# Layer 0's and the third layer's output projections in split operands, weights streamed for every block, and a bias table spread from DRAM to DRAM

## The reference

```python
# layer 0
o_a = rms_norm(diff_attention(..., rel_bias[:, :A_HEADS]), subln_g) * (1.0 - lam_init)
o_b = dsa_attention(..., rel_bias[:, A_HEADS:], top_k)
mix = jnp.concatenate([o_a, o_b], axis=-1)
return x + (mix * jax.nn.silu(gate)) @ w_o          # e_w_o, 1024 x 1024
# third layer (second block)
y_f = fourier_mix(u_f, w_fourier[l], b_fourier[l])
y_a = windowed_gqa(q, k, v, rel_bias, sink[l])
mixed = jnp.einsum('bse,ed->bsd', jnp.concatenate([y_f, y_a], axis=-1), w_out[l])
x = x + g1 * mixed
```

## Time and profile before

| | us |
|---|---|
| runs without a profile, median of 3 | 2521.23 |
| lowest and highest | 2519.8 and 2523.14 |
| the profiled execution, whole | 2521.95 |
| its span | 2520.0 |
| PE busy in it | 2331.1 |

### The profile page before, as it was taken

How to read it: one execution, slowest core, us unless ns; L and a number is a source line. 1 busy time by engine, 2 the same in 40 slices (tenths; PEclk the granted TensorE clock), 3 DMA queues, 4 the chain that set the end, 5 groups by cost and what they waited for, 6 DMA issues and landing times. The chain is left out here.

```text
span 2520.0 us, 35443 instructions
## 1 busy us (share of the span) xinstructions
PE 2331.1 (93%) x13159; PEld 1785.8 (71%) x13159; DVE 1737.0 (69%) x3255; ACT 1341.5 (53%) x2161; POOL 666.3 (26%) x586
## 2 busy tenths in 40 slices
PE   7789999899998999999998989989992999999998
PEld 6476887555655987777777878766661888888886
DVE  4899998768773325666776355336656888888886
ACT  5445312455554375556655242445443877777774
POOL 2345320111110000767678400002315121122210
PEclk9989999799998999999999989989995999999999
DMA  4232221210102332233333331211116999999995
GB/s 151 34 69 59 84 76 56 79 51 30 47 26 84 113 76 62 75 87 84 84 113 95 124 142 38 89 63 35 34 52 256 389 387 392 390 383 384 384 395 182
DMA packets 171320, 362.40 MB, mean 144 GB/s; under 512 B 44056, under 2 KB 91880, under 8 KB 171152
## 3 DMA queue, kind: packets, MB, share of 16 engines
q1 hardware_dynamic: 147344, 308.52, 33.7%
q0 software_dynamic: 23504, 51.48, 8.2%
q10 hardware_dynamic: 304, 0.15, 0.0%
HBM read 321.23 MB, written 38.82 MB: 143 GB/s over the span
## 5 line engine op out<-in xcount | busy, mean ns | idle before, releaser
L994 ACT ACTIVATE a_pT<-ps 128x512 f32<-128x512 f32 (+3 forms) x176 | 79.8, 484 | 181.6 <-PE ps L872 180.3
L1904 DVE MAX8 l_best<-sel 128x8 f32<-128x640 f32 (+5 forms) x176 | 162.8, 925 | 6.1
L1905 DVE MATCH_REPLACE8 sel<-l_best,sel 128x640 f32<-128x640 f32 (+5 forms) x176 | 159.5, 906 | 0.0
L3660 POOL DMA_INDIRECT out_dram<-m_q,e_token x15 | 34.0, 2266 | 447.4 <-DVE m_q L3858 447.4
L1006 ACT ACTIVATE a_p<-ps,a_stat 128x384 f32<-128x384 f32 (+7 forms) x192 | 129.0, 673 | 19.6 <-DVE a_stat L1085 13.7
L2659 ACT ACTIVATE l_lat<-ps,h_stat 128x384 f32<-128x384 f32 (+7 forms) x128 | 94.2, 740 | 76.9 <-DVE h_stat L2849 40.0
L919 PE MATMUL ps<-l_wo,a_mixT 128*128 128x512 f32 x256 | 119.9, 594 | 0.9 <-DVE a_y L2043 0.9
L2239 POOL TENSOR_TENSOR ada_acc<-ada_acc,ada_w 128x384 f32<-128x384 f32 x112 | 116.8, 1042 | 8.8
L2669 ACT ACTIVATE h_pT<-ps 128x512 f32<-128x512 f32 (+2 forms) x192 | 83.5, 490 | 58.9 <-PE ps L2542 58.9
L3489 DVE TENSOR_TENSOR x_w2l<-x_raw,x_w2h 128x4096 fp32r<-128x4096 f32 x23 | 101.8, 4425 | 18.4 <-ACT x_w2h L3481 18.4
L3489 DVE TENSOR_TENSOR x_w1l<-x_raw,x_w1h 128x4096 fp32r<-128x4096 f32 x23 | 101.8, 4425 | 16.1 <-ACT x_w1h L3481 16.1
(11 more groups left out here) (700 smaller groups left out, 7029.6 us busy)
## 6 DMA issues: line engine op xcount, KB each, us to landing
x_raw<-in_w_gate SPq DMA_DIRECT2D x25, 2048.0 KB, 11.5
x_raw<-in_w_down SPq DMA_DIRECT2D x24, 2048.0 KB, 10.9
x_raw<-in_w_up SPq DMA_DIRECT2D x23, 2048.0 KB, 11.9
ada_w<-in_w_ada POOLq DMA_DIRECT2D x64, 384.0 KB, 3.8
m_ufT<-in_w_up SPq DMA_DIRECT2D x9, 2048.0 KB, 12.3
m_ufT<-in_w_down SPq DMA_DIRECT2D x8, 2048.0 KB, 13.0
l_raw<-in_e_w_in SPq DMA_DIRECT2D x28, 512.0 KB, 4.0
m_ufT<-in_w_gate SPq DMA_DIRECT2D x7, 2048.0 KB, 10.4
```

The source lines that it names most:

```text
L1904: link(nc.vector.max(best[:], line))
L1905: link(nc.vector.match_replace(line, best[:], line, TAKEN))
```

## The change

Four things.

1. *The table of biases.* SP writes the 20 rows to a small DRAM tensor `rel_rows_d`, and then five DMAs of four heads each repeat them from DRAM to DRAM (`spread_rows`). Three are issued before the loads of QA1, G0 and G1, two between the stores of the first two strips of w_o and the gate stores. POOL issues none.
2. *Layer 0's w_o is split once and put in DRAM.* Four strips O0 to O3 of 256 columns of `e_w_o` go through the same raw tiles, ACT and POOL as the other strips, have no groups on PE, and are stored as high and low halves (1 MB each) to `wo_d`. The gate strips G2 and G3 come before KA0 now.
3. *Layer 0's pieces in split operands* (`StreamedOut`). For each block SP loads 16 units of 512 KB (high and low part of one piece's weights) into a ring of seven; three fp32r matmuls a piece. The left side is split in two halves a block, each with a copy on ACT and a subtraction on DVE. POOL now loads the x rows and stores the result rows.
4. *Chunks 0 to 3 of the third layer in split operands.* The weights are split in the Fourier stage (four copies on ACT, four subtractions on DVE); the left side with a copy on ACT and a subtraction on DVE for each block.

The core of the diff:

```diff
+    def store_out(e, n):
+        e.wait_ge(pr.lows, 2 * pr.place[OUT[n]] + 2)
+        for part, x in enumerate(out_room):
+            e.dma_start(t.wo_d[n // 2, :, :, part, n % 2 * 256:n % 2 * 256 + 256].rearrange("c p n -> p c n"), x[:].bitcast(F32)).then_inc(wo_out, 16)
+    def rows_to_dram(e):
+        e.wait_ge(tables.ready, 2)
+        e.dma_start(t.rel_rows_d[0:12], t.bias_rows[0:12, :]).then_inc(rows_sent, 16)
+        e.dma_start(t.rel_rows_d[12:20], t.bias_rows[32:40, :]).then_inc(rows_sent, 16)
+    def spread_rows(e, n):
+        table, h = divmod(4 * n, 12)
+        e.wait_ge(rows_sent, 32)
+        e.dma_start((t.rel1_d, t.rel2_d)[table][h:h + 4],
+                    t.rel_rows_d[4 * n:4 * n + 4, :].unsqueeze(1).broadcast_to([4, P, REL_LEN])).then_inc(rel_out[table], 16)
...
-            for i in (VA1, KB, QA0, QA1, G0, G1, KA0):
+            rows_to_dram(e)
+            pr.load(e, VA1)
+            pr.load(e, KB)
+            pr.load(e, QA0)
+            for n, i in enumerate((QA1, G0, G1)):
+                spread_rows(e, n)
                 pr.load(e, i)
-            gate.store(e, 0)
-            pr.load(e, KA1)
-            gate.store(e, 1)
+            for n, (out, later) in enumerate(zip(OUT, (G2, G3, KA0, KA1))):
+                pr.load(e, out)
+                pr.load(e, later)
+                store_out(e, n)
+                if n < 2:
+                    spread_rows(e, 3 + n)
+                gate.store(e, n)
...
-                    if n % 3 == 0 and n // 3 - 3 < len(PIECES):
-                        rel_piece(e, *PIECES[n // 3 - 3])
...
+class StreamedOut:
+    RING, HALF, UNITS = 7, KD // 2, 2 * KD
+    def load(self, e, at, n, h, c):
+        g = self.UNITS * n + KD * h + c
+        if g == 0:
+            e.wait_ge(self.wo_out, 128)
+        if g >= self.RING:
+            half, chunk = divmod(g - self.RING, KD)
+            self.unit_done(e, at, half // 2, half % 2, chunk)
+        i, _ = self.place(n, h, c)
+        e.dma_start(self.ring[i][:].bitcast(F32), self.t.wo_d[h, c]).then_inc(self.unit_in[i], 16)
+    def pe(self, e, n, h, c):
+        if h == 0 and c % self.HALF == 0:
+            e.wait_ge(self.mix_lows, 2 * n + c // self.HALF + 1)
+        i, times = self.place(n, h, c)
+        e.wait_ge(self.unit_in[i], 16 * times)
+        high, low = self.ring[i][:, 0, :], self.ring[i][:, 1, :]
+        for part, (x, w) in enumerate(((self.mix_h, high), (self.mix_h, low), (self.mix_l, high))):
+            last = self.nc.tensor.matmul(self.t.ps[:, 7, :], x[:, c, :], w, start=c == part == 0, stop=c == KD - 1 and part == 2)
...
+            for n in range(NB):
+                for q in range(split.UNITS):
+                    split.load(e, at, n, *divmod(q, KD))
+                    if q in (4, 6) and n + 1 < NB:
+                        at.load_gate(e, n + 1, q // 2 - 2, t.gateT_d)
...
+                    at.store(e, n - 1, t.x1_d)
+                    if n + 1 < NB:
+                        load_rows(e, n + 1)
...
+                for c in {1: (0, 1), 2: (2, 3)}.get(p, ()):
+                    e.wait_ge(wo_in, 32)
+                    nc.scalar.activation(wo_high[:, c, :], wo[:, c, :], ACT.Copy).then_inc(wo_highs, 1)
```

More of the change, by code:

```diff
@@ L915, in pe_pieces @@
                 self.chunk_ready(e, n, c)
-            if self.split and c >= self.split.FIRST:
+            if self.split:
                 last = self.split.pe(e, n, h, c)
@@ L1207, with __init__ @@
     FIRST = KD // 2
-    def __init__(self, k, t, raw):
+    def __init__(self, k, t, first, fixed, still):
         self.nc, self.t = k.nc, t
-        self.raw = [x.rearrange("p (c n) -> p c n", n=D) for x in raw]
-        self.high, self.low = (k.sb(f"w_wo{part}", [P, KD // 2, D], F32R) for part in "hl")
+        self.first_high, self.first_low = first
+        self.fixed, (self.fixed_h, self.fixed_l) = fixed, still
+        scope = k.scope
+        self.high = k.sb("w_woh", [P, KD // 2, D], F32R)
+        with ExitStack() as under:
+            k.scope = under
+            self.raw = k.sb("w_wo_raw", [P, KD // 2, D])
+        k.scope = scope
+        self.low = k.sb("w_wol", [P, KD // 2, D], F32R)
         self.mix_h, self.mix_l = (k.sb(f"w_mix{part}", [P, KD // 2, P], F32R) for part in "hl")
@@ L1243, in act @@
             e.wait_ge(self.raw_in[u // 2], 16)
-            self.nc.scalar.activation(self.high[:, u, :], self.raw[u // 2][:, u % 2, :], ACT.Copy).then_inc(self.highs, 1)
+            self.nc.scalar.activation(self.high[:, u, :], self.raw[:, u, :], ACT.Copy).then_inc(self.highs, 1)
         elif u % at.per == 0:
             self.act_mix(e, at, u // at.per - 1)
+        if u % at.per == at.per - 1:
+            n = u // at.per
+            if n:
+                e.wait_ge(self.fixed_used, n)
+            self.nc.scalar.activation(self.fixed_h[:], self.fixed(at.order[n]), ACT.Copy).then_inc(self.fixed_highs, 1)
     def dve(self, e, at, u):
@@ L1270, in __init__ @@
         self.pick = k.sb("r_pick", [P, EXPERTS])
+        scope = k.scope
+        with ExitStack() as under:
+            k.scope = under
+            self.under_shift = [k.sb(f"w_fixed{part}", [P, KD // 2, P], F32R) for part in "hl"]
+        k.scope = scope
         self.shift = k.sb("r_shift", [P, KD, P])
@@ L1444, in layer0 @@
             early = IndexRoom(k)
+        with ExitStack() as later:
+            k.scope = later
+            k.sb("l0_qi_pad", [P, 4, SEQ])
+            out_room = [k.sb(f"l0_wo_{part}", [P, KD, 256], F32R) for part in "hl"]
         k.scope = persist
@@ L1812, in _ @@
             e.dma_start(bias[:, :, :], offset_bias(t.rel1_d, range(12), P, 2 * P)).then_inc(b_in, 16)
-            pr.load(e, G2)
-            pr.load(e, G3)
-            gate.store(e, 2)
-            gate.store(e, 3)
         @block.gpsimd
```

190 lines of the change are left out of this document (134 added, 56 removed).

## The result

The changed kernel takes 2529.93 us in the median of 15 runs (2523.66 to 2534.64), the kernel before, on the same chips, 2521.31 (15 runs, 2516.31 to 2526.22). The ratio is 1.0033, interval 1.0025 to 1.0041: slower by a third of a per cent, where 2510 was forecast and the range ended at 2526. The profiled execution took 2526.13 us, with a span of 2524.3.

What follows compares the result with a forecast made beforehand. PE was taken as the limit in layer 0's and the third layer's attention, DVE's top-k as the projection's floor. +6 - 8.5 - 9.5 + 0.5 = -11.5 from 2521.95 gave 2510; range 2500 to 2516, with rivals 2493 to 2526.

Steps and rivals of the forecast that it cites:

- Table pieces leave POOL: Layer 0 projection: weights of strip KB land sooner, PE gains 26.5 us, by itself worth only 3.0.
- DVE's 429.3: Layer 0 projection: DVE's last top-k ends at 429.3 us, a floor that no gain of PE goes under.
- Strips of w_o in the projection: Layer 0 projection: late gate stores cost PE 32.5 us; PE ends at 438.3, the projection costs 6 us more.
- Rival B: Projection: gate stores wait longer, from a spread of about 19 us on; at 24.6, +24 and 2528 in all; chance 0.17.
- A: Projection: the spread is quick or its wait covered; -3 instead of +6, 2501 in all; chance 0.20.
- Layer 0's output pieces: Layer 0 attention: shorter split pieces give 12 us, copies take 5, the tail gives 1.6; -8.5 in all.
- two subtractions on DVE (0.68): Layer 0 block changes: part of the copies' cost, 1.3 us each with ACT's copies; 7 blocks at 0.7, minus 5.
- +3 if block changes eat the rest: Layer 0 attention: the slower bound of the step put at -8.5 us.
- Tail: End of layer 0's attention: sixteen shorter pieces give 2.6 us, POOL issuing the last store costs about 1; net 1.6.
- I cost it at nothing; its cover is that lead: Layer 0 attention's weight stream: seven ring places lead by 19 us on the mean, 13 in small blocks; cost nothing.
- Rival D: Layer 0 attention: the ring runs dry in small blocks, 0.5 us in 16 units, +8, 2518; chance 0.05.
- Third layer and Fourier: Third layer attention: 64 shorter pieces less new copies, -9.5 us; Fourier stage: ACT's four copies, +0.5.

Runs made afterwards that it cites:

- e2: Changed kernel, but SP issues each gate store as soon as due and the table spreads last: 2523.32 us, ratio 1.001 to the kernel before.
- e8: Changed kernel with POOL subtracting low halves, gate stores when due, SP issuing the last store, last half product in float32: 2515.15 us.
- e9: Changed kernel with POOL's addition waiting, gate stores when due, SP's last store, last half product in float32 with loads in order of need: 2505.85 us.
- e10: Kernel before plus the third layer's part and the table spread by SP from DRAM; no streamed weights: 2510.12 us, ratio 0.9949.
- e11: Changed kernel, but the left side is split for the first block alone and reused: 2511.62 us in one round, loop 336.9.
- e1: Changed kernel, but POOL's addition of x waits for DVE's first low-half subtraction of the next block: 2518.42 us, ratio 0.9992 to the kernel before.
- e12: Changed kernel, but POOL's addition of x is replaced by a MEMSET of the same shape: loop 343.1 us, whole time 2515.8 in one round.
- e4: Changed kernel, but the last block's pieces 7 to 15 reload no weights: 2522.33 us, ratio 0.9999 to the kernel before.
- e6: Changed kernel, but SP instead of POOL issues the store of the last block's rows: 2527.99 us, ratio 1.0025 to the kernel before.
- e3: Kernel before with the third layer's part of the change alone: 2512.29 us, ratio 0.9962.

## Why the prediction was wrong

**Table pieces leave POOL.** The mechanism held (KB in 2.8 us, no gap at 136). Of the 26.5 us of PE's gain, 22 are there: PE ends at 410 where nothing holds it (e2, e8, e9, e10) and at 432.3 before. Of the 4.5 that are missing about 3 lie in a new short gap: in the kernels with the table spread by SP, PE stands 1.5 us before 174 to 177, and in the changed kernel the granted clock is 0.72 from 174 to 180. The 3.0 us that this was to be worth alone are not: DVE's 429.3 was taken as fixed, and in e10 DVE ended at 433.7, held up by POOL as the loop is.

**Strips of w_o in the projection.** Right in mechanism and place. The loss of PE was put at 32.5, it is 436.9 - 410 = 27; the gain was 4.5 too large as well, so the errors nearly cancel, and 438.3 became 436.9: the sum is closer than its terms by luck. The spread, taken at 13, costs 11. Rival B didn't come: it needed 19. Nor did A: it needed a quick spread, on all 16 engines, and there were four.

**Layer 0's output pieces.** This is the step that failed. Its gain in the units was right (12 said, 11.7 in e11), and the copies' own cost nearly so (5 said, 6.4). What the step left out is in its sentence "two subtractions on DVE (0.68)": the duration was taken from the third layer and carried to a place where POOL adds 128x1024 of x at just that moment. There it is 2.7 us, six times, with PE behind it: 11.6 us (e1, e12). The rows that gave the 0.68 held the warning, and I did not look at their neighbours. POOL's addition stands there too; the instruction of DVE just ahead of the subtraction is held up by it, and the subtraction starts as it ends. In the trace of before, POOL's additions in layer 0, then the third layer: DVE's copies there, and one block change:
```profile
L2001 POOL TENSOR_TENSOR a_y<-a_y,l_xb x7: 2346/2350/2357, 527.5 to 781.2; 128x1024 f32<-128x1024 f32 x7
...
L1108 DVE COPY a_over<-a_stat x29: 226/227/2268, 1693.1 to 1861.6; 128x128 f32<-128x128 f32 x29
...
1749.55 2.35 POOL L3353 TENSOR_TENSOR m_ufT<-m_ufT,w_xb 128x1024 f32<-128x1024 f32 x1
1749.72 2.26 DVE L1108 COPY a_over<-a_stat 128x128 f32<-128x128 f32 x1
1751.91 0.68 DVE L1239 TENSOR_TENSOR w_mixl<-a_mixT,w_mixh 128x512 fp32r<-128x512 f32 x1
```
Median 0.23, longest 2.27, at six block changes: a duration whose longest is ten times its median asks for its neighbours. The copy reads one SBUF tile, so the clash is not one of instructions with two SBUF operands alone. The old layer 0 had no long operation of DVE that started at that moment, so its rows gave only clean ones. The bound of the step was "+3 if block changes eat the rest"; the loop alone reached +6.3.

**Tail.** Also failed: -1.6 was said, +7.6 came. "I cost it at nothing; its cover is that lead" holds in the loop, where PE never waited for the ring, and not in the tail, which the sentence did not look at: sixteen pieces in 11 us ask for 750 GB/s, the queue gave 407. e4 gives its price, 7.0 us, of which the three waits are 1.15 + 1.69 + 1.56 = 4.4 and most of the rest is the low clock behind them; e6 gives 3.1 for the store by POOL, where about 1 was booked. So the step as a whole missed by 22.4 us (-8.5 said, +13.9 measured), and the runs hold nearly all of it: 11.6 for the clash, 7.0 for the dry ring, 2.1 for the store, 1.4 for the copies. Rival D had the mechanism (a dry ring), but in the wrong place.

**Third layer and Fourier.** -9.5 said, -9.4 measured, and again -9.5 in e3; Fourier +0.5 said, -1.4 measured, and no run was made on that.

Profile against profile the change costs 4.2 us, by the medians 8.6. The stages above sum to 4.1. The rest stays open: the profiled execution of the changed kernel lies 3.8 below its median, first scores vary from 435.8 to 440.5 in the seven other kernels whose projection is the same, and the stage of layer 2 takes 767.3 here but 770 to 772 in seven of the ten other kernels with streamed weights (mostly in its attention). No run was made on it.

## What to carry over

A duration may be carried to another place only with its neighbours: look what POOL reads at the moment at which a DVE instruction starts, at the old place and at the new one, and look at the longest, not the median, of its kind. Held up here were DVE instructions with two SBUF operands (0.69 to 2.7 us), but a copy and a TENSOR_SCALAR with one as well. A streamed operand has to be priced where the consumer is fastest, which is the tail, and there the order of loads on one queue must be the order of need. Where PE is given back time ahead of a stage whose end another engine sets, expect none of it, and ask what the earlier PE moves beside that engine.

## What was not expected of the hardware

- DVE's blocked time counts as its busy time: 2.73 us for 0.69 of work, no wait in any view.
- The block is nearly complete, not a slowdown in proportion: in the six cases DVE ended 0.54 to 0.56 us after POOL, whether it had begun 0.11 or 0.25 after it; beside a MEMSET of POOL it lost nothing.
- A DVE copy of 128x128 from one SBUF tile took 2.26 us instead of 0.23 beside POOL's addition, and a TENSOR_SCALAR of 128x640 2.20 instead of 0.49.
- A 512 KB store issued by POOL took 3 us longer until the next layer could start than one issued by SP (8.8 against 5.8), though it landed only 0.3 us later after its issue.
- Six microseconds with PE busy 2.1 of them were followed by 1.2 GHz for 5 us, and waits of 4.4 us cost 7.
